# First mixer reordered with its attention mask added in PSUM, and a Fourier product folded in half both ways

## The reference

```
# first block, mixer
h = rms_norm(x, norm1_g);  q, k, v, xr, xg, xc = split(h @ w_in)      # 512,512,512,256,256,512 columns
q, k = rms_norm per head of 64 (8 heads)
y_a: z = q k^T / 8;  mask = s < t
     log_keep = where(mask, log_sigmoid(-z), 0);  suffix = reverse cumsum(log_keep) - log_keep
     w = where(mask, exp(log_sigmoid(z) + suffix), 0);  y_a = w @ v
y_b: xr = conv4(xr);  gates = sigmoid(xr @ blocks + b);  linear scan;  * gelu(xg)
y_c: u = val * sigmoid(gate);  u = conv31(u);  silu(layer_norm(u)) @ pw_w + pw_b
x = x + concat(rms_norm(y_a), rms_norm(y_b), rms_norm(y_c)) @ w_out
# second block, mixer: 512 of 1024 columns go through fourier_mix, four groups of 128 channels
out = fft2(f, axes=(positions, channels of the group), norm='ortho').real
```

## Time and profile before

| what | value |
|---|---|
| median of 3 runs (lowest, highest) | 2061.33 us (2059.81, 2066.96) |
| the profiled execution | 2055.64 us, span 2053.9 us |
| busy: PE, DVE, ACT, POOL | 1757.2, 616.5, 480.8, 207.7 us |
| mean granted TensorE clock | 0.925 |

### The profile page before, as it was taken

The page is one execution under the profiler, slowest core; times in us unless marked ns, Lnnn a source line. Parts: engine busy times, 40 slices in busy tenths (PEclk is TensorE's granted clock), DMA queues, the critical chain, the costliest instruction groups (busy, mean ns, idle before and its releaser), DMA issues.

```text
span 2053.9 us, 21389 instructions
## 1 busy us (share of the span) xinstructions
PE 1757.2 (86%) x8530; PEld 889.4 (43%) x8530; DVE 616.5 (30%) x1132; ACT 480.8 (23%) x818; POOL 207.7 (10%) x236
## 2 busy tenths in 40 slices
PE   4999666785999999999779998997499989999980
PEld 2454333343444555455335545963333333333330
DVE  1220453313321321212259933642321111111104
ACT  2311333421331211211158511331111111111111
POOL 0000231000111111111000013100011111111100
PEclk9999788897999999999979999999699999999995
DMA  9466101044999999999490080045298999999974
GB/s 362 165 247 211 41 0 41 0 146 151 380 390 398 413 403 402 402 411 409 200 343 1 11 120 9 33 183 206 95 349 319 388 379 404 394 368 381 424 309 153
DMA packets 93994, 515.78 MB, mean 251 GB/s; under 512 B 22333, under 2 KB 28061, under 8 KB 69320
## 3 DMA queue, kind: packets, MB, share of 16 engines
q1 hardware_dynamic: 82696, 497.01, 62.7%
q0 software_dynamic: 11200, 17.39, 2.5%
HBM read 506.64 MB, written 27.05 MB: 260 GB/s over the span
## 4 chain that ended last, share of the span: by engine, by line
PE 70%; DMA 13%; DVE 9%; ACT 3%; issue 2%; SPq 2%; POOL 1%; POOLq 0%; DVEq 0%; ACTq 0%
PE bank L800 20%; PE bank L816 9%; PE bank L463 8%; PE bank L438 8%; DMA ring<-in_w_up 7%; PE bank L762 3%; PE bank L787 3%; DMA ring<-in_w_down 2%; PE bank L431 2%; PE bank L827 1%; PE bank L714 1%; PE bank L521 1%; PE bank L1129 1%; PE bank L659 1%; PE bank L1137 1%
## 5 line engine op out<-in xcount | busy, mean ns | idle before, releaser
L800 PE MATMUL bank<-ring,arena 128*64 128x512 f32 x1104 | 503.6, 610 | 34.0 <-DMA ring<-in_w_up 30.8
L802 PE MATMUL bank<-ring,arena 128*64 128x512 f32 x1104 | 503.9, 611 | 0.0
L800 PEld LDWEIGHTS bank<-ring,arena 128*64 128x64 f32 x1104 | 149.2, 140 | 325.3 <-issue 317.8
L438 PE MATMUL bank<-arena,ring 128*128 128x512 f32 x576 | 254.0, 598 | 8.1 <-DVE arena L2035 8.1
L2284 DVE TENSOR_TENSOR arena<-arena,bank 64x512 f32<-64x512 f32 x70 | 48.3, 690 | 689.1 <-ACT arena L1666 689.1
L816 PE MATMUL bank<-ring,arena 128*64 128x512 f32 x552 | 251.6, 598 | 3.3 <-DMA ring<-in_w_down 2.8
L818 PE MATMUL bank<-ring,arena 128*64 128x512 f32 x552 | 251.6, 598 | 0.0
L1666 ACT ACTIVATE arena<-bank 64x512 f32<-64x512 f32 x70 | 41.2, 589 | 559.8 <-PE bank L802 559.8
L438 PEld LDWEIGHTS bank<-arena,ring 128*128 128x128 f32 x576 | 109.0, 192 | 141.5 <-issue 132.5
L1345 POOL DMA_INDIRECT arena<-xnd,smalli x70 | 67.2, 961 | 914.9 <-PE bank L787 599.7
L802 PEld LDWEIGHTS bank<-ring,arena 128*64 128x64 f32 x1104 | 149.2, 140 | 0.0
(11 more groups left out here) (414 smaller groups left out, 1862.6 us busy)
## 6 DMA issues: line engine op xcount, KB each, us to landing
ring<-in_w_gate SPq DMA_DIRECT2D x63, 2048.0 KB, 12.8
ring<-in_w_up SPq DMA_DIRECT2D x63, 2048.0 KB, 17.7
ring<-in_w_down SPq DMA_DIRECT2D x63, 2048.0 KB, 18.9
ring<-in_w_mod SPq DMA_DIRECT2D x12, 2048.0 KB, 15.5
ring<-in_w_in SPq DMA_DIRECT2D x10, 2048.0 KB, 19.4
ring<-in_w_out SPq DMA_DIRECT2D x4, 2048.0 KB, 11.2
arena<-yd SPq DMA_DIRECT2D x16, 512.0 KB, 7.6
arena<-in_w_in SPq DMA_DIRECT2D x2, 2048.0 KB, 11.8
```

Of the source, the lines that this page charges most:

```text
L438: mm = pe.matmul(b[:, 0:n], w[:, k, col:col + P], ap[:, k, :], start=(k == 0), stop=(k == KD - 1))
L800: pe.matmul(GU[0:CAP, :], x, wg_[:, c, :], start=(c == 0), stop=(c == KD - 1), skip_group_check=True)
L802: mm = pe.matmul(GU[CAP:2 * CAP, :], x, wu_[:, c, :], start=(c == 0), stop=(c == KD - 1), skip_group_check=True)
```

## The change

In the first mixer the side branches' projections come first, ahead of q and k; the unit order of the weights (`U_IN`, `U_MOD`) follows. x is loaded in four pieces ahead of the matrices and parameters, its squares are added in pairs by DVE, and four instead of eight matmuls sum them. The convolutions, the scan and the norms of the side branches run between the projections of q, k and v. In the attention `scores` adds a tile `far` (-1e9 at and under the diagonal) to the four diagonal tiles of z through the identity matrix; POOL's two steps are gone, and `decays` and `values` wait for DVE's and ACT's results directly. The order of a head's steps on PE is changed, with scores two heads ahead. `project` begins with the side branches' chunks (4 to 7) while the norm of y_a is made. In the second mixer the two halves of the positions are added and subtracted by DVE (256 columns each), cosines and sines are multiplied for even and odd bins apart, for bins up to 256 alone, and DVE makes the mirrored bins from the two.

```diff
-        U_IN, U_MOD, U_OUT = [1, 5, 10, 15, 16], [0, 2, 3, 4, 6, 7, 8, 9, 11, 12, 13, 14], 17
+        U_IN, U_MOD, U_OUT = [2, 8, 13, 0, 1], [3, 4, 5, 6, 7, 9, 10, 11, 12, 14, 15, 16], 17
...
-            pe.wait_ge(S("silu_c"), 1)
-            modulation(0, 1)
-
-            colsum(C, "ss_x", M["ones"], [sq8[:, k, :] for k in range(KD)], "sq_x", KD)
-            pe.wait_ge(S("h_ready"), KD)
+            colsum(C, "ss_x", M["ones"], [sq8[:, k, :] for k in range(0, KD, 2)], "sq_pairs", KD // 2)
+
+            w = use(U_IN[3])
+            b = V.deal(pe, "xr0")
+            for k in range(KD):
+                pe.wait_ge(S("h_ready"), k + 1)
+                mm = pe.matmul(b[:, :], w[:, k, 0:P], xT[:, k, :], start=(k == 0), stop=(k == KD - 1))
+            mm.then_inc(V.full, 1)
+            feature(V, "xr1", w, P, xT)
+            for c in range(2):
+                feature(C, f"xg{c}", w, 256 + P * c, xT)
+            used(U_IN[3], C, "xg1")
+
+            w = use(U_IN[4])
+            for c in range(2):
+                feature(C, f"cg{c}", w, 256 + P * c, xT)
+            for c in range(2):
+                feature(V, f"cv{c}", w, P * c, xT)
+            used(U_IN[4], V, "cv1")
+
+            pe.wait_ge(S("xconv"), 2)
+            pe.wait_ge(S("parts1"), 16 * 4)
+            for c in range(2):
+                for g in range(2):
+                    b = C.deal(pe, f"lru{c}{g}")
+                    pe.matmul(b[:, :], lbd[:, 2 * g + c, :], xconv[:, c, :], start=True, stop=True)\
+                      .then_inc(C.full, 1)
 
             for n in range(8):
                 if n == 4:
-                    modulation(1, 4)
+                    pe.wait_ge(S("silu_c"), 1)
+                    modulation(0, 5)
                 w = use(U_IN[n // 4])
                 feature(V, f"qk{n}", w, P * (n % 4), xT)
                 if n:
                     colsum(C, f"ss_qk{n - 1}", M["blk"], [sq2[:, (n - 1) % 2, :]], "sq_qk", n)
                 used(U_IN[n // 4], V, f"qk{n}")
-
-            modulation(4, 8)
+            modulation(5, 9)
+
             w = use(U_IN[2])
             for s in range(TT):
...
                     colsum(C, "ss_qk7", M["blk"], [sq2[:, 1, :]], "sq_qk", 8)
+                    colsum(C, "ss_b", M["ones"], [sqB[:, c, :] for c in range(2)], "sq_y", 2)
+                    modulation(9, 10)
+                if s == 1:
+                    colsum(V, "mu", M["ones"], [dwo[:, c, :] for c in range(2)], "dwconv", 2)
+                    modulation(10, 11)
+                if s == 2:
+                    colsum(C, "ss_ln", M["ones"], [sq2[:, c, :] for c in range(2)], "sq_ln", 2)
+                    modulation(11, 12)
...
+
+            pe.wait_ge(S("ln_silu"), 2)
+            for e in range(2):
+                b = C.deal(pe, f"pw{e}")
+                for c in range(2):
+                    mm = pe.matmul(b[:, :], pw[:, c, P * e:P * e + P], lnx[:, c, :], start=(c == 0), stop=(c == 1))
+                mm.then_inc(C.full, 1)
...
                 for c in (0, 1, 3, 2):
-                    mm = pe.matmul(zpart(z, c), qk[r:r + HD, 4 + h // 2, P * c:P * c + P],
-                                   qk[r:r + HD, h // 2, P * c:T], start=(c != 3), stop=True,
+                    pe.matmul(zpart(z, c), qk[r:r + HD, 4 + h // 2, P * c:P * c + P],
+                              qk[r:r + HD, h // 2, P * c:T], start=(c != 3), stop=False,
+                              skip_group_check=True)
+                for c in range(4):
+                    mm = pe.matmul(zpart(z, c)[:, 0:P], M["ident"], far, start=False, stop=True,
                                    skip_group_check=True)
                 mm.then_inc(S("z_ready"), 1)
...
-                pe.wait_ge(S("sp_ready"), h + 1)
+                pe.wait_ge(S("sp_raw"), 3 * (h + 1))
...
-                pe.wait_ge(S("w_ready"), h + 1)
+                pe.wait_ge(S("w_raw"), 3 * (h + 1))
...
+            pe.wait_ge(S("far"), 1)
             scores(0)
+            pe.wait_ge(C.free, C.at("pw1"))
+            pe.wait_ge(S("sq_y"), 4)
+            for c in range(2):
+                mm = pe.matmul(psum[7][:, :], M["ones"], sqC[:, c, :], start=(c == 0), stop=(c == 1))
+            mm.then_inc(S("ss_c"), 1)
+            scores(1)
             for h in range(NH):
-                if h + 1 < NH:
-                    scores(h + 1)
+                decays(h)
                 if h:
                     values(h - 1)
-                decays(h)
+                if h + 2 < NH:
+                    scores(h + 2)
             values(NH - 1)
-            pe.wait_ge(S("o_taken"), NH // 2)
             pe.wait_ge(S("w_raw"), 3 * NH)
 
...
                 for n in range(2):
...
+
...
+                    def part(t, ks, last):
+                        for k in ks:
+                            mm = pe.matmul(banks[t][:, :], yT(k)[:, P * t:P * t + P], w[:, k, :],
+                                           start=(k == 4), stop=(last and k == ks[-1]), skip_group_check=True)
+                        if last:
+                            mm.then_inc(V.full, 1)
+
+                    if n == 0:
+                        pe.wait_ge(S("outA_ready"), 4)
                         for t in range(TT):
-                            for k in range(k0, k1):
-                                mm = pe.matmul(banks[t][:, :], yt[:, k, P * t:P * t + P], w[:, k, :],
-                                               start=(k == 0), stop=(k == KD - 1), skip_group_check=True)
-                            if k1 == KD:
-                                mm.then_inc(V.full, 1)
-                    used(u + n, V, f"{tag}{n}{TT - 1}")
-
-            project(U_OUT, "outA", yT, [(0, 4, 4), (4, 6, 6), (6, 8, 8)])
+                            part(t, range(4, 8), False)
+                            if t == 1:
+                                pe.wait_ge(S("o_taken"), NH // 2)
+                                colsum(C, "ss_a", M["ones"], [sqA[:, k, :] for k in range(4)], "sq_y", 8)
+                        pe.wait_ge(S("outA_ready"), 8)
+                        for t in range(TT):
+                            part(t, range(4), True)
+                    else:
+                        for t in range(TT):
+                            part(t, (4, 5, 6, 7, 0, 1, 2, 3), True)
+                    used(U_OUT + n, V, f"outA{n}{TT - 1}")
...
                 if g == 0:
                     pe.wait_ge(V.free, V.at(f"ab{TT - 1}0"))
                     pe.wait_ge(C.free, C.at(f"ab{TT - 1}1"))
-                for s in range(TT):
-                    pe.matmul(b[:, :], AB[:, s, g, 0:P], w[:, s, :], start=(s == 0), stop=False)
-                    mm = pe.matmul(b[:, :], AB[:, s, g, P:2 * P], w[:, TT + s, :], start=False, stop=(s == TT - 1))
+                for odd, (c0, s0, s1) in enumerate(BINS):
+                    for s in (2 * odd, 2 * odd + 1):
+                        pe.matmul(b[:, c0:s0], AB[:, s, g, 0:P], w[:, s, 0:s0 - c0], start=(s == 0), stop=(s % 2 == 1),
+                                  skip_group_check=True)
+                        mm = pe.matmul(b[:, s0:s1], AB[:, s, g, P:2 * P], w[:, TT + s, 0:s1 - s0], start=False,
+                                       stop=(s % 2 == 1), skip_group_check=True)
                 mm.then_inc(V.full, 1)
 
...
         def _(sp):
+            x_cols = a["xT"].rearrange("(c p) t -> p c t", p=P)
+            for j in range(TT):
+                sp.dma_start(xT[:, 2 * j:2 * j + 2], x_cols[:, 2 * j:2 * j + 2]).then_inc(S(f"y_in{j}"), 16)
+            sp.dma_start(mats[:, :, :], a["mats"].rearrange("p (n f) -> p n f", f=P)).then_inc(S("params"), 16)
             sp.dma_start(par[:, :], a["par"]).then_inc(S("params"), 16)
-            sp.dma_start(mats[:, :, :], a["mats"].rearrange("p (n f) -> p n f", f=P)).then_inc(S("params"), 16)
-            sp.dma_start(xT, a["xT"].rearrange("(c p) t -> p c t", p=P)).then_inc(S("x_in"), 16)
 
...
-
-            for h in range(NH + 1):
-                if h < NH:
-                    pool.wait_ge(S("sp_raw"), 3 * (h + 1))
-                    for c in range(4):
-                        d = kpart(spb[h % 2], c)[:, 0:P]
-                        last = pool.tensor_tensor(d, d, M["lt"], ALU.mult)
-                    last.then_inc(S("sp_ready"), 1)
-                if h:
-                    pool.wait_ge(S("w_raw"), 3 * h)
-                    for c in range(4):
-                        d = kpart(wb[(h - 1) % 2], c)[:, 0:P]
-                        last = pool.affine_select(out=d, in_=d, pattern=[[1, P]], compare_op=ALU.is_gt,
-                                                  fill=0.0, base=0, channel_multiplier=-1)
-                    last.then_inc(S("w_ready"), 1)
-
             def experts(m):
 
...
+            def qk_norm(n):
+                dve.wait_ge(C.free, C.at(f"ss_qk{n}"))
+                STT(qk[:, n, :], qk[:, n, :], gq8 if n < 4 else pcol("gk"), root[:, n % 2, :], ALU.mult, ALU.mult)\
+                    .then_inc(S("qk_ready"), 1)
+
```

(28 more changed lines are left out.)

353 lines of the change are left out of this document (170 added, 183 removed).

## The result

The kernel after takes **1944.56 us** (median of 4 runs, 1941.8 to 1950.82), the kernel before beside it 2060.57: a ratio of 0.9447, with a 95% interval of 0.9399 to 0.9495. A second measurement of the same kernel gave 1943.67 (6 runs, 1935.37 to 1957.18), ratio 0.945 (0.9421 to 0.948). The forecast was 1950 in a range of 1934 to 1984. The profiled execution took 1950.82 us, 104.8 us less than the profiled one of before, where the sum said 111.1; between the medians of this measurement lie 116.0.

A forecast was written before the change was run, and what follows sets the result against it. PE was held to be unfilled in three of the stages changed, waiting for POOL in the attention, and full in Fourier. Terms summed to -111.1 us: 2055.64 to 1944.5, plus 5.7 for the median, 1950 us; range 1934 to 1984.

The forecast's parts named there:

- A: Start: PE's first projection comes at 22.4 instead of 36.44 us, a gain of 14.0 us, bounds 3 us either way.
- B: Projections up to the first scores: added matmuls and a modulation unit cost 14.8 us, bounds +13 and +25.
- C: Attention: PE sets the pace at 10.3 us per head, 86.4 us instead of 137.3, a gain of 50.9 us.
- D: Gap after the attention: its work moves elsewhere and the norm of y_a is covered; -43.3 us, bounds -43.3 and -36.
- E: Output projection: 59.3 us instead of 58.0, a cost of 1.3 us.
- F: Fourier stage: four calls of 7.1 us in all instead of 27.5, less 1.3 given back; -19.0 us, bounds -20.3 and -9.
- tie at `mu`: End of projections: DVE's last taps ready after 27 us, PE's covering work 27.5 us; 1 us of waiting taken.
- DVE is late in the projections: Rival, projections: a delay of 15 us, with all 20 last taps bare, gives 1965 us; chance 0.15.
- Fourier bound by its inverse: Rival, Fourier stage: the inverse's cover falls from 6.9 to 1.8 us, costing 10 us in all, 1960 us; chance 0.12.
- The heads don't overlap: Rival, attention: 15.1 us bare per head makes eight heads 121 us, +35 us, 1985 us; chance 0.08.
- The clock stays down: Rival, attention: half of its 84 us at 1.2 GHz costs 42 us more, 1992 us; chance 0.03.
- Slower: Rival, 22 to 350 us: side branches' work makes PE run at 1.2 GHz; gain gone if 111 us run so; chance 0.01.

The follow-up runs named there:

- e12: The kernel after, unchanged, measured once more: median 1943.67 us (6 runs), ratio 0.945; profiled execution 1957.18 us.
- e9: The kernel before with only the heads' order changed (the copy of a pair moves along), GpSimd's steps and taps kept: attention 93.6 us, one execution 2017.62 us.
- e4b: The kernel after with the old order of heads and GpSimd's masking and clearing, taps still in the projections: attention 98.7 us, median 1958.17 us.
- e10: The kernel after with old head order, GpSimd's two steps and 12 one-input VectorE operations added behind each head (4 behind the last): attention 102.3 us, one execution 1959.21 us.
- e5: The kernel after with the sum for the norm of y_a ahead of the whole output projection: one execution, 1959.42 us.
- e6: The kernel after with five modulation units split, four before the fifth piece of q and k, one before the sixth: median 1947.02 us, ratio 0.9477.
- e4: The kernel after with the old order of heads, mask still in the bank, no GpSimd, no taps in the attention: attention 103.3 us, one execution 1966.89 us.

## Why the prediction was right

The time, the sign and most of the mechanism came out as forecast, and each stage that the sum has a term for within 4 us:

| step | forecast | after | again |
|---|---|---|---|
| A first projection at | 22.4 | 20.8 | 22.3 |
| B to the first scores | 186.5 | 188.7 | 190.4 |
| C attention | 86.4 | 87.6 | 87.6 |
| D gap | 0 | 0 | 0 |
| E output projection | 59.3 | 59.7 | 59.8 |
| F Fourier stage | 23.3 | 22.2 | - |
| from `project` to Fourier (no term) | 797.4 | 802.8 | 803.4 |

**The largest miss is one for which the sum has no term.** The profiled execution lies 6.3 us over the sum's 1944.5: 1.6 less in A, 2.2 more in B, 1.2 in C, 0.4 in E, 1.1 less in F, and 5.4 more on the way from `project` to the Fourier stage. The prediction names longer stages of experts as a sign of being wrong, and on this point it was: I had them pass the gain on unchanged. e12 shows the same, but six of the eight changed kernels with this front do not (795.0 to 798.5 us). Luck helped the number: 5.7 us were added to the sum because the profile of before lay 5.7 under its median, but the profile of after lies 6.3 over its own. So 1950 meets the profile's 1950.82 by chance, and the median, 1944.56, is 5.4 under it.

**A.** The sum of squares began at 12.15 and took 5.1 us, its records 0.85 us apart up to 14.9 and 0.43 from there, where I had 6.4 of an engine that had done nothing. The root's table load was followed by its two activations with nothing between:

```profile
17.27 1.28 ACT L1459 ACT_TABLE_LOAD   x1 [6.88 <-PE bank L440]
18.56 0.69 ACT L1460 ACTIVATE arena<-bank,smallf 128x512 f32<-128x512 f32 x1
19.28 0.63 ACT L1461 ACTIVATE arena<-arena 128x512 f32<-128x512 f32 x1
```

That is 2.6 us, as the row of before had it, and again with no room for the drain of some 1.38 us that the Trainium skill (ScalarE: Activation LUTs, What ACT_TABLE_LOAD costs) adds.

**B is the term of the sum that was most mis-sized**, by 2.2 to 4 us. The feared tie at `mu` did not occur: the last tap ended at 181.7 and PE came to `mu` at 184.8. What I left out is a wait for VectorE at the fifth unit of the modulation (2.15 us; ScalarE's square root for the scan had kept VectorE 1.55 us ahead of it), and that behind this wait PE fell to 1.2 GHz for a few us in eight of ten profiles. Over the ten profiles with this order (two of them with the modulation split) the stage took 183.3 to 193.3 us, and PE's busy time in it 179.6 to 187.1 through the same instructions: its clock, 1.00 to 0.96, made most of the difference.

**C** came within 1.2 us, but for a reason that I had half wrong. (Its bare 0.8 and 1.4 us add up to 2.2, not 2.4; measured, 2.1.) I wrote that "the waits there were POOL's", and the rows name it. Yet with GpSimd's steps kept, and all else changed, the attention takes 85.4 us. Why they waited so long before shows in the timelines of before around one long wait, VectorE first, then ScalarE (a softplus's last step, an exponential), then GpSimd:

```profile
255.56 0.69 DVE L2095 COPY arena<-bank 128x512 f32<-128x512 f32 x1 [17.43 <-PE bank L714]
256.17 6.25 DVE L2078 SCALAR_TENSOR_TENSOR arena<-arena,par 128x512 f32<-128x512 f32 x8
262.46 1.62 DVE L2092 SCALAR_TENSOR_TENSOR arena<-bank,arena 128x512 f32<-128x512 f32 x3
```
```profile
253.80 1.36 ACT L1581 ACTIVATE arena<-arena,smallf 128x1280 f32<-128x1280 f32 x1
260.48 1.36 ACT L1593 ACTIVATE arena<-bank 128x512 f32<-128x512 f32 x3 [5.31 <-PE bank L702]
```
```profile
264.16 3.47 POOL L1323 TENSOR_TENSOR arena<-arena,mats 128x128 f32<-128x128 f32 x4 [15.21 <-DVE arena L2092]
267.60 2.77 POOL L1329 TENSOR_SCALAR_AFFINE_SELECT arena<-arena 128x128 f32<-128x128 f32 x4
...
280.22 1.03 POOL L1329 TENSOR_SCALAR_AFFINE_SELECT arena<-arena 128x128 f32<-128x128 f32 x4 [6.57 <-ACT arena L1593]
```

VectorE stood 17.4 us at the copy of a pair of heads, which waits for PE's `values`, with eight taps behind it. When `values` came, the taps ran first, and VectorE's step for the next head (L2092), due at 255.16 when ScalarE had its softplus, ended at 264.08. GpSimd has the triangle of that head ahead of the clearing of the one before, in its program's order; both then ran beside taps, 3.47 us for 1.69 and 2.77 for 1.03, and PE's `values` waited for the clearing until 270.42. So a wait of PE's went round through VectorE and GpSimd back to PE, every second head: three of the five waits for the clearing, 21.5 of the 29.6 us, stand behind such a copy. The first (5.6 us) has taps ahead of L2092 and no copy.

Had the steps kept their short times, the clearing would have ended at 264.16 + 1.69 + 1.03 = 266.9, 1.5 us after PE was ready at 265.4, not 5. Had L2092 been in time, the triangle would have ended at 255.16 + 1.62 + 3.47 = 260.3 and the clearing, from the end of the exponential, at 261.84 + 2.77 = 264.6, before PE was ready, even at the long times. So by these estimates the late L2092 is the larger part of this wait. e9 agrees: there GpSimd is as slow as before (722 and 592 ns), in another order and with a copy that hardly waits, and after the second head PE waits at most 0.74 us for it.

**What stays open:** how the 38.6 us between before and e4b divide between the copy's place and the shared port. In every run in which the taps left, or their kind changed, the copy had moved as well; a kernel before with only the copy one head later would tell, and it was not run. e10 gives an estimate. One of its heads, GpSimd and then `values`:

```profile
238.14 2.35 POOL L1353 TENSOR_TENSOR arena<-arena,mats 128x128 f32<-128x128 f32 x4 [6.65 <-DVE arena L2166]
240.56 1.75 POOL L1359 TENSOR_SCALAR_AFFINE_SELECT arena<-arena 128x128 f32<-128x128 f32 x4
242.89 2.37 PE L747 MATMUL bank<-arena 128*64 128x512 f32 x8
```

With the 3.47 and 3.10 us that the two steps took beside taps, the clearing would end at 244.7, 1.8 us after PE was ready; six such heads are 11 us. By that the larger part would be the copy's place, but no run shows it.

What the 38.6 us consist of is plain from windows and waits: 27.9 us less of waiting for GpSimd (37.2 to 9.3) and 10.6 less of busy PE (91.35 to 80.70, with 2.0 for the norm of y_c in it), since its clock went from 0.78 to 0.95.

**D** held, though one of its figures is wrong (16 matmuls are 13.7 us without the sum's 3.4, and its 17.2 has both), and e5 shows that it hung on the cover: with nothing over the norm of y_a, 10 us come back. **E** held. **F** was forecast 1.1 us too dear: the give-back of 1.3 us for bare copies did not occur, four calls of 1.79 us and their inverses followed each other with PE busy 22.17 of 22.20 us.

**The rivals.** *DVE is late in the projections*: only the 2.15 us. *Fourier bound by its inverse*: no. *The heads don't overlap*: they do, with at most 2.1 us of waits. *The clock stays down*: 0.96 in the attention, and 1.00 in e6; the second failure mode of the Trainium skill (TensorE: Matmul & The Clock Gate, A second HAM failure mode), of a kernel that goes round its banks with short idles, did not show. *Slower*: no.

## What to carry to other kernels

The engine that a wait names is the last link, not the cause: before its work is moved away, look at what delayed its input (here a copy that waits for PE, with unneeded work behind it in VectorE's queue) and at whether its instructions take longer in this stretch than elsewhere. Two edits that each remove the same knot don't add up, so price them in both orders; of the changes to this attention one, the mask in the bank, was worth nothing. Spare work belongs behind what others wait for, and a wait that depends on the bottleneck belongs at the end of what is ready.

## What the hardware showed

- GpSimd's 128x128 multiplication took 479 ns beside an idle VectorE, 722 beside its two-input taps and 604 beside one-input operations; its clearing 291, 592 and 445.
- A wait of PE of 2.15 us at one place cost 1.3 to 1.7 us more behind it in eight of ten profiles (64 records of the modulation took 3.26 to 3.62 us for 1.93) and at most 0.15 in two (e4b, e6). Of e4's eight waits of 1.45 us five cost nothing behind them, and three 1.6 to 3.3 us.
- The first 20 us of the experts fell into two kinds, clock 0.91 to 0.93 or 0.69 to 0.77, and the way to the Fourier stage, 800 us, kept the difference: 795.0 to 798.5 us or 800.3 to 803.4. Less data moved early (183 to 192 GB/s for 217 to 225) and a DMA share of 1.00 behind it fit a delay that can't be caught up, but PE is as full there (328.00 of 328 us), and no run separates the two.
